# A hybrid decoder layer: where the halves of the projection's weights are stored

## The chip, the core and the metric

The program runs on one core of a Trainium2 chip. A core has a matrix engine (TensorE, PE in the rows, with its weight loads as PEld), a vector engine (VectorE, DVE), a scalar engine (ScalarE, ACT), GpSimd (POOL) and SyncE (SP), which in this kernel issues every DMA. Each engine runs its own list of instructions in order and waits for the others through semaphores. The metric is the device time of one execution in microseconds (us). Before the change it was 2645.74 us (median of 3 runs, 2643.93 to 2646.36).

## What is computed

One decoder layer over 2048 prompt rows and 8 sequences of 8 sample rows, all in float32, width 1024. Cut to its matrix products and what lies between them:

```
h   = rmsnorm(x, g_pre_mix)
z, q, k, v, glow, og = split(h @ w_in)              # 1024 x 2064
pool_out = pool_mixer(z, ...)                       # trailing windows 2, 4, 8, 16, minus z, per-group map
gla_out  = gla_mixer(q, k, v, log_sigmoid(glow @ w_gk2 + b) / 16, og, state)   # gated linear attention, chunks of 64
x   = x + rmsnorm(concat(pool_out, gla_out) @ w_o)
u, g = split(rmsnorm(x) @ w_up)                     # 1024 x 5632
x   = x + rmsnorm((gelu(causal_conv3(g)) * u) @ w_down)
x   = x + (p @ w_ple) * sigmoid(x @ w_ple_gate)
```

## The kernel before

The rows are cut into six tiles of 320, 384, 384, 384, 384 and 256 rows (tile 0 has 256 prompt rows and the 64 sample rows). The tiles go through the layer one after the other. A product of float32 accuracy is made from three matmuls (L1619, L1620, L1621): a matrix is split into a high half that TensorE takes exactly (`fp32r`) and a low half, the rest, and high*high, high*low and low*high are added up in PSUM.

The weights come as units of 128 partitions by 1024 words (512 KB), one for each block of 128 output columns. `UNITS` lists them all in the order in which TensorE takes them: for each tile 16 units `in` (in0 to in15), then, for the tile before, the first `ple` unit and three `gate` units, the eight `o` units, the second `ple` unit and five more `gate` units, 44 `up` units and 24 `down` units. Tile 0's `gate` units thus stand between tile 1's units. Four slots in SBUF hold the units; unit n goes to slot n % 4. A slot has two buffers: `stage`, over which `w_lo` lies in the same place, and `w_hi`.

For a plain unit SP loads the block into `stage`, ACT copies it to `w_hi` (L719, which rounds), DVE subtracts (L1133) and writes `w_lo` over `stage`, and TensorE waits for `lo_made`. For the 24 units `in` and `gate` of tile 0 both halves are then stored in DRAM (`kept_hi`, `kept_lo`), and all later tiles load the two halves in place of the block; for these units ACT and DVE have nothing to do, and TensorE waits for the landing of both (`halves_ready`).

SP's order is that of `load_unit(n)`. If the slot's former unit n-4 is to be kept, it first issues the two stores of that unit (`keep_unit`, L461 and L462); then it waits until TensorE has finished unit n-4 (`end_tick`, a count in `ticks`), then until the stores have landed (`keeping`), and only then issues the load of unit n. The stores of unit n-4 thus always go out right behind the load of unit n-1.

ACT and DVE go through the same list of units. At step n ACT first takes unit n-1's result out of PSUM (`finish`), then splits unit n+2 (`make_hi(n + 2)`), waiting for its landing, and only behind that does the step's own work: for tile units 3 to 9 `decay` (exponentials for one level of the attention's scores), at 9 and later `copy_v`, at 12 `copy_kd`, at the first `ple` unit `copy_out`, `square_out` and the evacuation of the `ple` results. DVE begins step n with `make_lo(n + 1)`. TensorE multiplies each level's operands (`scores`, L1678 and L1683) behind units in4 to in10, makes the chunks' states (`sum_state`, L1733) behind in12 and the chunks' outputs (L1748, L1754) behind in13 to in15.

Of the kernel before, what the change touches and what calls it, by code (L numbers as in the profile page):

```python
# [7 lines left out]
F32 = mybir.dt.float32  # L8
F32R = mybir.dt.float32r
U8 = mybir.dt.uint8  # L10
ALU = mybir.AluOpType
ACT = mybir.ActivationFunctionType

P = 128
D = 1024
KD = D // P
# [28 lines left out]
SLOTS = 4  # L45
# [15 lines left out]
def plan():  # L61

    units, outs, ticks = [], [], []

    def ple(t, s):
        units.append((t, "ple", s))
        for m in range(4 * s, 4 * s + 4):
            outs.append((t, "ple", m))
            ticks.append((t, "ple", m))

    def full(t, kind, m):
        for table in (units, outs, ticks):
            table.append((t, kind, m))

    for t in range(NT):
        for s in range(16):
            full(t, "in", s)
            if s >= 8 and s - 8 < chunks(t) + (TILES[t][2] > 0):
                outs.append((t, "v", s - 8))
        if t:  # L80
            ple(t - 1, 0)
            for m in range(EARLY_GATES):
                full(t - 1, "gate", m)
        for m in range(KD):
            full(t, "o", m)
        if t:
            ple(t - 1, 1)
            for m in range(EARLY_GATES, KD):
                full(t - 1, "gate", m)
        for m in range(2 * NF):  # L90
            full(t, "up", m)
        for m in range(3 * KD):
            units.append((t, "down", m))
            ticks.append((t, "down", m))
            if m % 3 == 0:
                outs.append((t, "down", m // 3))
    for s in range(2):
        ple(LAST, s)
    for m in range(KD):
        full(LAST, "gate", m)  # L100
    return units, outs, ticks


UNITS, OUTS, TICKS = plan()

KEPT = [unit for unit in UNITS if unit[0] == 0 and unit[1] in ("in", "gate")]
KEPT_NO = {unit[1:]: j for j, unit in enumerate(KEPT)}
HALVES = [unit[0] > 0 and unit[1:] in KEPT_NO for unit in UNITS]
SPLITS = list(itertools.accumulate(not halves for halves in HALVES))
UNIT_NO = {name: n for n, name in enumerate(UNITS)}  # L110
OUT_NO = {name: n for n, name in enumerate(OUTS)}
TICK_NO = {name: n for n, name in enumerate(TICKS)}
# [33 lines left out]
def hybrid_layer(nc, x_prompt, x_sample, state_pool, state_gla, state_conv, p_prompt, p_sample, packed,  # L146
# [4 lines left out]
    with ctx:  # L151
# [4 lines left out]
        def region(words):  # L156
            o = base[0]
            base[0] += (4 * words + 31) // 32 * 32
            assert base[0] <= top, (base[0], top)
            return o  # L160

        def at(name, shape, offset, dtype=F32):
            return nc.alloc_sbuf_tensor_at(name, shape, dtype, offset=offset)

        def own(name, shape, dtype=F32):
            n = mybir.dt.size(dtype)
            for s in shape[1:]:
                n *= s
            return at(name, shape, region((n + 3) // 4), dtype)
# [41 lines left out]
        slot_at = [region(KD * P) for _ in range(SLOTS)]  # L211
        stage = [at(f"stage{s}", [P, KD, P], slot_at[s]) for s in range(SLOTS)]
        w_lo = [at(f"w_lo{s}", [P, KD, P], slot_at[s], F32R) for s in range(SLOTS)]
        w_hi = [own(f"w_hi{s}", [P, KD, P], F32R) for s in range(SLOTS)]

        xr = [own(f"xr{n}", [P, KD, TM]) for n in range(2)]
        h_hi = own("h_hi", [P, KD, TM], F32R)
# [94 lines left out]
        def sem(name):  # L312
            return ctx.enter_context(nc.semaphore(name))
# [7 lines left out]
        landed = [sem(f"landed{s}") for s in range(SLOTS)]  # L321
        kept = [sem(f"kept{s}") for s in range(SLOTS)]
        hi_made, lo_made, ticks = sem("hi_made"), sem("lo_made"), sem("ticks")
# [71 lines left out]
        def exact(ap):  # L395
            return ap.bitcast(F32)
# [30 lines left out]

        def landing(n):

            return landed[n % SLOTS], 16 * sum(1 + HALVES[k] for k in range(n % SLOTS, n + 1, SLOTS))  # L430

        def keeping(n):
            return kept[n % SLOTS], 32 * sum(UNITS[k] in KEPT for k in range(n % SLOTS, n + 1, SLOTS))

        def tick(name):
            return ticks, TICK_NO[name] + 1
# [1 line left out]
        def end_tick(unit):  # L438
            t, kind, m = unit
            return tick((t, "ple", 4 * m + 3)) if kind == "ple" else tick(unit)  # L440

        def parts_of(unit):
            return DOWN_PARTS[unit[2] % 3][1] if unit[1] == "down" else KD
# [5 lines left out]
        def _(sp):  # L449
            def source(unit):  # L450
                t, kind, m = unit
                if kind == "down":
                    first_k, parts = DOWN_PARTS[m % 3]
                    return w_down_units[m // 3, :, first_k:first_k + parts, :]
                return {"in": w_in_units, "o": w_o_units, "up": w_up_units, "ple": w_ple_units,
                        "gate": w_gate_units}[kind][m]

            def keep_unit(n):
                s, j = n % SLOTS, KEPT_NO[UNITS[n][1:]]
                sp.wait_ge(lo_made, SPLITS[n])  # L460
                sp.dma_start(kept_hi[j], exact(w_hi[s][:, :, :])).then_inc(kept[s], 16)  # L461
                sp.dma_start(kept_lo[j], exact(w_lo[s][:, :, :])).then_inc(kept[s], 16)  # L462

            def load_unit(n):
                unit = UNITS[n]
                if n >= SLOTS:
                    if UNITS[n - SLOTS] in KEPT:
                        keep_unit(n - SLOTS)
                    sp.wait_ge(*end_tick(UNITS[n - SLOTS]))
                    if UNITS[n - SLOTS] in KEPT:  # L470
                        sp.wait_ge(*keeping(n - SLOTS))
                if HALVES[n]:
                    s, j = n % SLOTS, KEPT_NO[unit[1:]]
                    sp.dma_start(exact(w_hi[s][:, :, :]), kept_hi[j]).then_inc(landed[s], 16)
                    sp.dma_start(exact(w_lo[s][:, :, :]), kept_lo[j]).then_inc(landed[s], 16)
                    return
                dst = stage[n % SLOTS][:, 0:parts_of(unit), :]
                if unit[1] == "ple":
                    dst = dst.rearrange("p (k c) d -> p k (c d)", k=2)
                sp.dma_start(dst, source(unit)).then_inc(landed[n % SLOTS], 16)  # L480
# [36 lines left out]

            load_first_x()
            load_unit(0)
            sp.dma_start(const[:, 0:C_GK], packed[:, 0:C_GK]).then_inc(const_loaded, 16)  # L520
            load_unit(1)
            sp.dma_start(const[:, C_GK:C_ALL], packed[:, C_GK:C_ALL]).then_inc(tables_loaded, 16)
            load_unit(2)
            zs = state_pool[0].rearrange("b t (g c) -> (b t g) c", g=POOLG).rearrange("(q p) c -> p q c", p=120)
            sp.dma_start(z_state_tok[:, :, :], zs).then_inc(states_loaded, 16)
# [8 lines left out]
            for n in range(SLOTS, len(UNITS)):  # L534
                t, kind, m = UNITS[n]
# [169 lines left out]
        def _(act):  # L705
# [4 lines left out]
            def make_hi(n):  # L710
                for k in range(hi_next[0], min(n + 1, len(UNITS))):
                    one_hi(k)
                hi_next[0] = max(hi_next[0], n + 1)

            def one_hi(n):
                if n < len(UNITS) and not HALVES[n]:
                    s, parts = n % SLOTS, parts_of(UNITS[n])
                    act.wait_ge(*landing(n))
                    act.activation(w_hi[s][:, 0:parts, :], stage[s][:, 0:parts, :], ACT.Copy).then_inc(hi_made, 1)  # L719

            def root(out, ps, t, of=D):
                w = width(t)
# [247 lines left out]
            for n, (t, kind, m) in enumerate(UNITS):  # L970
# [78 lines left out]
                if kind == "up":  # L1049
                    f = m // 2  # L1050
# [64 lines left out]
        def _(dve):  # L1115
# [8 lines left out]
            def make_lo(n):  # L1124
                for k in range(lo_next[0], min(n + 1, len(UNITS))):
                    one_lo(k)
                lo_next[0] = max(lo_next[0], n + 1)

            def one_lo(n):
                if n < len(UNITS) and not HALVES[n]:  # L1130
                    s, parts = n % SLOTS, parts_of(UNITS[n])
                    dve.wait_ge(hi_made, SPLITS[n])
                    dve.tensor_tensor(w_lo[s][:, 0:parts, :], stage[s][:, 0:parts, :], exact(w_hi[s][:, 0:parts, :]),  # L1133
                                      ALU.subtract).then_inc(lo_made, 1)

# [334 lines left out]
            for n, (t, kind, m) in enumerate(UNITS):  # L1470
# [69 lines left out]
                if kind == "up":  # L1540
                    f = m // 2
# [60 lines left out]
        def _(pe):  # L1602
# [244 lines left out]
                y_turned.did(last, t, m)  # L1847

            def halves_ready(n):
                if HALVES[n]:  # L1850
                    pe.wait_ge(*landing(n))
                else:
                    pe.wait_ge(lo_made, SPLITS[n])

            def whole_unit(n, hi, lo, ready=None, between=None):
                t, kind, m = UNITS[n]
# [245 lines left out]
```

## Time and profile before

| | |
|---|---|
| median of the timed runs | 2645.74 us |
| the profiled execution's own time | 2644.32 us |
| its span in the trace | 2642.6 us |
| TensorE matmuls (PE) | 2579.1 us busy, 98% |
| weight loads (PEld) | 2515.4 us, 95% |
| VectorE (DVE) | 1581.9 us, 60% |
| ScalarE (ACT) | 1238.8 us, 47% |
| GpSimd (POOL) | 163.1 us, 6% |
| DMA | 428.54 MB, mean 162 GB/s |
| of it stored halves | 24 `kept_hi` and 24 `kept_lo`, 512 KB each |

How to read it: the span is one execution from first to last instruction. Busy shares are averages over stages that differ; a PE that is busy all the time may still run at half its clock, so the granted clock (PEclk, 1.00 is full) is read beside it. SPq is the queue on which SP issues DMAs; its rows begin when an instruction could be issued, after its waits. "idle 2.47 <-DVE ..." on a row says how long the engine stood still before it and what came last. Rows of the chain of waits follow the work that ended last back to its start.

### The profile page before, as it was taken

What the parts mean: (1) busy time and instruction counts of PE and PEld (TensorE: products, weight loads), DVE (VectorE), ACT (ScalarE), POOL (GpSimd) and SP (SyncE); (2) the same over time, 40 slices, a digit from 0 to 9 for tenths busy, and PEclk for the clock granted to TensorE, in tenths of its full rate; (3) what the DMA queues carried; (4) which work ended last, traced back from release to release, by engine and by line L of the source; (5) the groups of instructions that cost most, each with busy time, mean ns of one, the idle gap of its engine ahead of it and who ended that gap; (6) DMA issues with size and microseconds to landing.
All of it is one profiled execution on the core that took longest, in us unless ns stands there. A gap on an engine that the chain in (4) does not pass through costs nothing.

```text
span 2642.6 us, 41219 instructions
## 1 busy us (share of the span) xinstructions
PE 2579.1 (98%) x16510; PEld 2515.4 (95%) x16510; DVE 1581.9 (60%) x2539; ACT 1238.8 (47%) x2036; POOL 163.1 (6%) x492
## 2 busy tenths in 40 slices
PE   7889999998999999999999999999999999999998
PEld 6779999998999999999999999999999999999998
DVE  5557764647664464766546476644557664557864
ACT  3345553365444335544533654452355444356553
POOL 3201100100000010000001000000100000010000
PEclk9889999999999999999999999999999999999999
DMA  7633546446434544443454444345444434756566
GB/s 213 220 116 128 175 140 195 160 160 206 150 127 118 182 169 145 167 152 126 119 190 163 151 153 151 127 117 193 168 152 151 142 122 119 246 181 216 186 181 210
DMA packets 126564, 428.54 MB, mean 162 GB/s; under 512 B 13246, under 2 KB 21606, under 8 KB 126374
## 3 DMA queue, kind: packets, MB, share of 16 engines
q1 hardware_dynamic: 126374, 425.91, 49.1%
q8 instruction: 132, 2.16, 0.3%
q14 instruction: 58, 0.48, 0.1%
HBM read 390.38 MB, written 35.48 MB: 161 GB/s over the span
## 4 chain that ended last, share of the span: by engine, by line
PE 92%; DMA 3%; DVE 2%; ACT 1%; issue 1%; POOL 1%; SPq 0%; DVEq 0%; POOLq 0%
PE G L1619 28%; PE G L1620 28%; PE G L1621 28%; DMA kept_lo<-w_lo 2%; PE X L1678 2%; PE X L1612 1%; PE X L1615 1%; DMA stage<-in_w_up_units_dram 1%; PE X L1748 1%; PE X L1733 1%; PE X L1800 1%; DVE w_lo L1133 0%; PE X L1779 0%; PE X L1754 0%; PE G L1612 0%
## 5 line engine op out<-in xcount | busy, mean ns | idle before, releaser
L1619 PE MATMUL G<-h_hi,w_hi 128*128 128x384 f32 (+2 forms) x3264 | 1070.7, 328 | 23.5 <-DVE w_lo L1133 11.4
L1620 PE MATMUL G<-h_hi,w_lo 128*128 128x384 f32 (+2 forms) x3264 | 1053.5, 323 | 0.0
L1621 PE MATMUL G<-h_lo,w_hi 128*128 128x384 f32 (+2 forms) x3264 | 1053.3, 323 | 0.0
L719 ACT ACTIVATE w_hi<-stage 128x1024 fp32r<-128x1024 f32 (+1 forms) x492 | 510.5, 1038 | 485.5 <-DMA stage<-in_w_up_units_dram 253.3
L1133 DVE TENSOR_TENSOR w_lo<-stage,w_hi 128x1024 fp32r<-128x1024 f32 (+1 forms) x492 | 588.0, 1195 | 210.0 <-ACT w_hi L719 209.6
L1619 PEld LDWEIGHTS G<-h_hi,w_hi 128*128 128x128 f32 x3264 | 619.2, 190 | 32.6 <-DVE w_lo L1133 13.6
L1620 PEld LDWEIGHTS G<-h_hi,w_lo 128*128 128x128 f32 x3264 | 619.3, 190 | 1.0
L1621 PEld LDWEIGHTS G<-h_lo,w_hi 128*128 128x128 f32 x3264 | 618.7, 190 | 0.0
L1619 PE MATMUL G<-y_hi,w_hi 128*128 128x384 f32 (+2 forms) x1056 | 346.3, 328 | 0.0
L1621 PE MATMUL G<-y_lo,w_hi 128*128 128x384 f32 (+2 forms) x1056 | 339.6, 322 | 0.0
L1620 PE MATMUL G<-y_hi,w_lo 128*128 128x384 f32 (+2 forms) x1056 | 339.5, 321 | 0.0
L1395 DVE SCALAR_TENSOR_TENSOR cg<-gx,const,cg 128x384 f32<-128x384 f32 (+1 forms) x264 | 151.5, 574 | 88.3 <-ACT cg L878 63.8
L1619 PEld LDWEIGHTS G<-y_hi,w_hi 128*128 128x128 f32 x1056 | 199.1, 188 | 4.0 <-issue 2.9
L1620 PEld LDWEIGHTS G<-y_hi,w_lo 128*128 128x128 f32 x1056 | 199.2, 189 | 1.1
L1621 PEld LDWEIGHTS G<-y_lo,w_hi 128*128 128x128 f32 x1056 | 199.0, 188 | 0.0
L1383 DVE TENSOR_TENSOR gx<-G,rms_up 128x384 f32<-128x384 f32 (+1 forms) x132 | 67.6, 512 | 198.4 <-PE G L1621 183.4
L1141 DVE TENSOR_TENSOR total<-total,sq 128x384 f32<-128x384 f32 (+2 forms) x126 | 65.9, 523 | 155.3 <-ACT sq L732 154.3
L885 ACT ACTIVATE cg<-cg 128x384 f32<-128x384 f32 (+2 forms) x132 | 66.0, 500 | 173.7 <-DVE cg L1395 141.5
L732 ACT ACTIVATE sq<-G 128x384 f32<-128x384 f32 (+2 forms) x84 | 39.0, 465 | 216.3 <-PE G L1621 216.3
L1619 PE MATMUL G<-xg_hi,w_hi 128*128 128x384 f32 (+2 forms) x384 | 128.9, 336 | 3.7 <-DVE xg_lo L1434 2.3
L1620 PE MATMUL G<-xg_hi,w_lo 128*128 128x384 f32 (+2 forms) x384 | 124.1, 323 | 0.0
L1621 PE MATMUL G<-xg_lo,w_hi 128*128 128x384 f32 (+2 forms) x384 | 124.1, 323 | 0.0
(225 smaller groups left out, 2553.8 us busy)
## 6 DMA issues: line engine op xcount, KB each, us to landing
stage<-in_w_up_units_dram SPq DMA_DIRECT2D x264, 512.0 KB, 3.5
w_hi<-kept_hi SPq DMA_DIRECT2D x120, 512.0 KB, 3.7
w_lo<-kept_lo SPq DMA_DIRECT2D x120, 512.0 KB, 4.7
stage<-in_w_down_units_dram SPq DMA_DIRECT2D x96, 448.0 KB, 3.3
stage<-in_w_o_units_dram SPq DMA_DIRECT2D x48, 512.0 KB, 3.5
stage<-in_w_down_units_dram SPq DMA_DIRECT2D x48, 512.0 KB, 3.5
kept_hi<-w_hi SPq DMA_DIRECT2D x24, 512.0 KB, 5.3
kept_lo<-w_lo SPq DMA_DIRECT2D x24, 512.0 KB, 6.1
```

The source lines that it names most:

```text
L719: act.activation(w_hi[s][:, 0:parts, :], stage[s][:, 0:parts, :], ACT.Copy).then_inc(hi_made, 1)
L732: squared.did(act.activation(out[:, 0:width(t)], src[:, 0:width(t)], ACT.Square), t, m)
L885: gelu_made.did(act.activation(c[:, 0:w], c[:, 0:w], ACT.Gelu_apprx_tanh), t, f)
L1133: dve.tensor_tensor(w_lo[s][:, 0:parts, :], stage[s][:, 0:parts, :], exact(w_hi[s][:, 0:parts, :]), ALU.subtract).then_inc(lo_made, 1)
L1141: added.did(dve.tensor_tensor(start[:, 0:w], start[:, 0:w], ring[:, m % 2, 0:w], ALU.add), t, m - 1)
L1383: last = dve.tensor_tensor(x[:, 2:2 + np_], G[b][:, 0:np_], rms_up[:, 0:np_], ALU.mult)
L1395: last = dve.scalar_tensor_tensor(c[:, 0:np_], x[:, k:k + np_], tap, c[:, 0:np_], ALU.mult, ALU.add)
L1612: return pe.transpose(out, in_, ident[0:n, 0:n])
L1619: pe.matmul(ps[:, 0:w], l_hi, r_hi[:, 0:w], start=start, stop=False)
L1620: pe.matmul(ps[:, 0:w], l_lo, r_hi[:, 0:w], start=False, stop=False)
L1621: return pe.matmul(ps[:, 0:w], l_hi, r_lo[:, 0:w], start=False, stop=stop)
L1678: last = pe.matmul(X[first + b][:, col:col + 64], opnd[n % 2][r, d, cols(c)], queries[n % 2][r, d, 64 * c:64 * c + 64], start=True, stop=True)
```

## The change

In tile 0 the `in` units store only `w_lo`. In tile 1 the `in` units load the whole block (from `w_in`) and the stored low half; the block goes into a new name `w_whole` for the place of `w_hi`, ACT rounds it in place, and SP stores `w_hi` from there. Tiles 2 to 5 load two halves as before. The `gate` units keep both halves in tile 0 as before. TensorE waits in tile 1's `in` units for `hi_made` rather than for the landing.

```diff
-KEPT = [unit for unit in UNITS if unit[0] == 0 and unit[1] in ("in", "gate")]
-KEPT_NO = {unit[1:]: j for j, unit in enumerate(KEPT)}
-HALVES = [unit[0] > 0 and unit[1:] in KEPT_NO for unit in UNITS]
-SPLITS = list(itertools.accumulate(not halves for halves in HALVES))
+KEPT_NO = {unit[1:]: j for j, unit in enumerate(unit for unit in UNITS if unit[0] == 0 and unit[1] in ("in", "gate"))}
+KEEP_LO = [unit[0] == 0 and unit[1:] in KEPT_NO for unit in UNITS]
+KEEP_HI = [unit[1:] in KEPT_NO and unit[0] == (1 if unit[1] == "in" else 0) for unit in UNITS]
+
+LOADS_LO = [unit[0] > 0 and unit[1:] in KEPT_NO for unit in UNITS]
+LOADS_HI = [lo and not hi for lo, hi in zip(LOADS_LO, KEEP_HI)]
+HIS_MADE = list(itertools.accumulate(not loaded for loaded in LOADS_HI))
+LOS_MADE = list(itertools.accumulate(not loaded for loaded in LOADS_LO))
...
-        w_hi = [own(f"w_hi{s}", [P, KD, P], F32R) for s in range(SLOTS)]
+        hi_at = [region(KD * P) for _ in range(SLOTS)]
+        w_hi = [at(f"w_hi{s}", [P, KD, P], hi_at[s], F32R) for s in range(SLOTS)]
+        w_whole = [at(f"w_whole{s}", [P, KD, P], hi_at[s]) for s in range(SLOTS)]
...
-            def keep_unit(n):
-                s, j = n % SLOTS, KEPT_NO[UNITS[n][1:]]
-                sp.wait_ge(lo_made, SPLITS[n])
-                sp.dma_start(kept_hi[j], exact(w_hi[s][:, :, :])).then_inc(kept[s], 16)
-                sp.dma_start(kept_lo[j], exact(w_lo[s][:, :, :])).then_inc(kept[s], 16)
+            def keep_halves(n):
+                s, name = n % SLOTS, UNITS[n][1:]
+                if KEEP_HI[n]:
+                    sp.wait_ge(hi_made, HIS_MADE[n])
+                    sp.dma_start(kept_hi[KEPT_NO[name]], exact(w_hi[s][:, :, :])).then_inc(kept[s], 16)
+                if KEEP_LO[n]:
+                    sp.wait_ge(lo_made, LOS_MADE[n])
+                    sp.dma_start(kept_lo[KEPT_NO[name]], exact(w_lo[s][:, :, :])).then_inc(kept[s], 16)
...
-                if HALVES[n]:
+                if LOADS_LO[n]:
                     s, j = n % SLOTS, KEPT_NO[unit[1:]]
-                    sp.dma_start(exact(w_hi[s][:, :, :]), kept_hi[j]).then_inc(landed[s], 16)
+                    if LOADS_HI[n]:
+                        sp.dma_start(exact(w_hi[s][:, :, :]), kept_hi[j]).then_inc(landed[s], 16)
+                    else:
+                        sp.dma_start(w_whole[s][:, :, :], source(unit)).then_inc(landed[s], 16)
                     sp.dma_start(exact(w_lo[s][:, :, :]), kept_lo[j]).then_inc(landed[s], 16)
...
             def one_hi(n):
-                if n < len(UNITS) and not HALVES[n]:
+                if n < len(UNITS) and not LOADS_HI[n]:
                     s, parts = n % SLOTS, parts_of(UNITS[n])
+                    whole = w_whole[s] if LOADS_LO[n] else stage[s]
                     act.wait_ge(*landing(n))
-                    act.activation(w_hi[s][:, 0:parts, :], stage[s][:, 0:parts, :], ACT.Copy).then_inc(hi_made, 1)
+                    act.activation(w_hi[s][:, 0:parts, :], whole[:, 0:parts, :], ACT.Copy).then_inc(hi_made, 1)
...
             def halves_ready(n):
-                if HALVES[n]:
+                if LOADS_HI[n]:
                     pe.wait_ge(*landing(n))
+                elif LOADS_LO[n]:
+                    pe.wait_ge(hi_made, HIS_MADE[n])
                 else:
-                    pe.wait_ge(lo_made, SPLITS[n])
+                    pe.wait_ge(lo_made, LOS_MADE[n])
```

SP, tile 0, from the store of unit in0 to the load of in5, before (the number at the end of `w_hi`, `w_lo`, `stage` and `w_whole` tells the slot):

```order
L461 DMA kept_hi<-w_hi_72 128x1024
L462 DMA kept_lo<-w_lo_68 128x1024
L480 DMA stage_64<-in_w_in_units_dram 128x1024
L461 DMA kept_hi<-w_hi_73 128x1024
L462 DMA kept_lo<-w_lo_69 128x1024
L480 DMA stage_65<-in_w_in_units_dram 128x1024
```

SP at the same place in the changed kernel (its lines are numbered anew: L472 is the store of `w_lo`, L492 the load):

```order
L472 DMA kept_lo<-w_lo_68 128x1024
L492 DMA stage_64<-in_w_in_units_dram 128x1024
L472 DMA kept_lo<-w_lo_69 128x1024
L492 DMA stage_65<-in_w_in_units_dram 128x1024
L472 DMA kept_lo<-w_lo_70 128x1024
```

Between two loads one store stands where two stood; this holds 16 times. SP, tile 1, the loads of units in3 to in5, before:

```order
L474 DMA w_hi_75<-kept_hi 128x1024
L475 DMA w_lo_71<-kept_lo 128x1024
L474 DMA w_hi_72<-kept_hi 128x1024
L475 DMA w_lo_68<-kept_lo 128x1024
L474 DMA w_hi_73<-kept_hi 128x1024
```

The same place in the changed kernel:

```order
L486 DMA w_whole_79<-in_w_in_units_dram 128x1024
L487 DMA w_lo_71<-kept_lo 128x1024
L469 DMA kept_hi<-w_hi_72 128x1024
L486 DMA w_whole_76<-in_w_in_units_dram 128x1024
L487 DMA w_lo_68<-kept_lo 128x1024
L469 DMA kept_hi<-w_hi_73 128x1024
L486 DMA w_whole_77<-in_w_in_units_dram 128x1024
```

The two loads of in4, in5 and so on now stand behind a store of `kept_hi`, for whose landing they wait; the 16 stores stand before the loads of in4 to in15, of the first `ple` unit and of three `gate` units. ACT, tile 1, steps 11 to 13, before:

```order
L802 ACTIVATE v_tok<-G 128x512
L771 ACTIVATE Z<-G 128x384
L806 ACTIVATE kd_tok<-X 128x512
L809 ACTIVATE kd_tok<-X 128x256
L972 ACT_TABLE_LOAD
L776 ACTIVATE ogT<-G 128x384 x2
L719 ACTIVATE w_hi_72<-stage_64 128x1024
```

The same steps in the changed kernel:

```order
L732 ACTIVATE w_hi_73<-w_whole_77 128x1024
L815 ACTIVATE v_tok<-G 128x512
L784 ACTIVATE Z<-G 128x384
L732 ACTIVATE w_hi_74<-w_whole_78 128x1024
L819 ACTIVATE kd_tok<-X 128x512
L822 ACTIVATE kd_tok<-X 128x256
L985 ACT_TABLE_LOAD
L789 ACTIVATE ogT<-G 128x384
L732 ACTIVATE w_hi_75<-w_whole_79 128x1024
L789 ACTIVATE ogT<-G 128x384
L732 ACTIVATE w_hi_72<-stage_64 128x1024
```

ACT has a copy of 1024 words a partition in each of tile 1's steps (16 in all), and `kd_tok` of step 12 stands behind the copy of in14. TensorE, VectorE and GpSimd have the same instructions in the same order in both kernels.

## Rows read from the trace of the kernel before

**Rows 1.** The page: TensorE, and the shares of the chain that ended last.

```profile
PE 2579.1 (98%) x16510; PEld 2515.4 (95%) x16510; DVE 1581.9 (60%) x2539; ACT 1238.8 (47%) x2036; POOL 163.1 (6%) x492
PE 92%; DMA 3%; DVE 2%; ACT 1%; issue 1%; POOL 1%; SPq 0%; DVEq 0%; POOLq 0%
```

**Rows 2.** Waits of SP's queue: total us, times, longest.

```profile
SPq L471 <- DMA kept_lo<-w_lo: 138.6, 24, 7.0
```

**Rows 3.** The chain from 28 to 140 us: start, length, what.

```profile
61.04 0.33 SPq L480
...
61.89 6.15 DMA kept_lo<-w_lo
68.11 0.33 SPq L480
```

**Rows 4.** Timeline of SP in tile 0: the loads of in4 and in14.

```profile
32.09 0.33 SPq L480 DMA_DIRECT2D stage<-in_w_in_units_dram  x1
...
103.74 0.33 SPq L480 DMA_DIRECT2D stage<-in_w_in_units_dram  x1
```

**Rows 5.** Timeline of TensorE in tile 0: the waits behind 58 us.

```profile
68.72 1.11 PE L1678 MATMUL X<-queries,opnd 64*128 64x64 f32 x16 [1.06 <-DVE queries L1209]
...
76.01 1.08 PE L1678 MATMUL X<-queries,opnd 64*128 64x64 f32 x8 [2.47 <-DVE queries L1209]
...
89.54 0.44 PE L1619 MATMUL G<-h_hi,w_hi 128*128 128x320 f32 x1 [2.47 <-DVE w_lo L1133]
...
109.98 2.25 PE L1733 MATMUL X<-v_tok,kd_tok 128*128 128x256 f32 x5 [4.95 <-issue]
```

**Rows 6.** Busy us by stretch, then PEclk (granted), DMA share, GB/s.

```profile
57.00:95.00 38.00, 31.31 (x231) 29.01 (x231) 20.16 (x42) 11.92 (x24) 0.00 (x0) 0.87 0.67 232
95.00:127.60 32.60, 27.59 (x195) 25.52 (x193) 18.07 (x43) 11.22 (x21) 15.06 (x19) 0.95 0.63 203
127.60:149.30 21.70, 20.09 (x104) 17.88 (x103) 6.77 (x13) 12.44 (x25) 0.00 (x0) 0.69 0.48 167
...
443.00:514.00 71.00, 70.25 (x515) 67.26 (x515) 41.19 (x64) 22.83 (x48) 7.79 (x10) 1.00 0.58 199
```

**Rows 7.** Timeline of ACT in tile 0, step 12.

```profile
108.08 1.06 ACT L719 ACTIVATE w_hi<-stage 128x1024 fp32r<-128x1024 f32 x1 [4.96 <-DMA stage<-in_w_in_units_dram]
...
109.52 0.36 ACT L809 ACTIVATE kd_tok<-X 64x256 f32<-64x256 f32 x1
```

**Rows 8.** DMA issues in 33:80, 125:170, 465:515 and 443.1:447.3 us: KB, us to landing.

```profile
kept_lo<-w_lo SPq DMA_DIRECT2D x7, 512.0 KB, 6.1
...
stage<-in_w_o_units_dram SPq DMA_DIRECT2D x7, 512.0 KB, 3.5
...
w_lo<-kept_lo SPq DMA_DIRECT2D x8, 512.0 KB, 4.7
...
w_lo<-kept_lo SPq DMA_DIRECT2D x1, 512.0 KB, 6.4
```

**Rows 9.** Timeline of SP in tile 1: loads of in3, in4 and the second gate unit.

```profile
443.17 0.32 SPq L474 DMA_DIRECT2D w_hi<-kept_hi  x1
443.54 0.43 SPq L475 DMA_DIRECT2D w_lo<-kept_lo  x1
447.34 0.32 SPq L474 DMA_DIRECT2D w_hi<-kept_hi  x1
...
527.59 0.33 SPq L480 DMA_DIRECT2D stage<-in_w_gate_units_dram  x1
```

**Rows 10.** Timeline of TensorE in tile 1: the chunks' states, the last quarter of `ple`.

```profile
514.75 2.75 PE L1733 MATMUL X<-v_tok,kd_tok 128*128 128x256 f32 x12
...
538.79 0.42 PE L1619 MATMUL G<-p_hi,w_hi 128*128 128x320 f32 x1 [0.98 <-ACT ple L924]
```

**Rows 11.** Timeline of ACT in tile 1: end of step 12, and the second gate unit's split.

```profile
511.28 0.38 ACT L809 ACTIVATE kd_tok<-X 128x256 f32<-128x256 f32 x1
...
533.88 1.05 ACT L719 ACTIVATE w_hi<-stage 128x1024 fp32r<-128x1024 f32 x1
```

More of the change, by code:

```diff
@@ L428, in landing @@
         def landing(n):
-            return landed[n % SLOTS], 16 * sum(1 + HALVES[k] for k in range(n % SLOTS, n + 1, SLOTS))
+            return landed[n % SLOTS], 16 * sum(1 + LOADS_LO[k] for k in range(n % SLOTS, n + 1, SLOTS))
         def keeping(n):
-            return kept[n % SLOTS], 32 * sum(UNITS[k] in KEPT for k in range(n % SLOTS, n + 1, SLOTS))
+            return kept[n % SLOTS], 16 * sum(KEEP_LO[k] + KEEP_HI[k] for k in range(n % SLOTS, n + 1, SLOTS))
         def tick(name):
@@ L466, in load_unit @@
                 if n >= SLOTS:
-                    if UNITS[n - SLOTS] in KEPT:
-                        keep_unit(n - SLOTS)
+                    keep_halves(n - SLOTS)
                     sp.wait_ge(*end_tick(UNITS[n - SLOTS]))
-                    if UNITS[n - SLOTS] in KEPT:
+                    if KEEP_LO[n - SLOTS] or KEEP_HI[n - SLOTS]:
                         sp.wait_ge(*keeping(n - SLOTS))
-                if HALVES[n]:
+                if LOADS_LO[n]:
                     s, j = n % SLOTS, KEPT_NO[unit[1:]]
-                    sp.dma_start(exact(w_hi[s][:, :, :]), kept_hi[j]).then_inc(landed[s], 16)
+                    if LOADS_HI[n]:
+                        sp.dma_start(exact(w_hi[s][:, :, :]), kept_hi[j]).then_inc(landed[s], 16)
+                    else:
+                        sp.dma_start(w_whole[s][:, :, :], source(unit)).then_inc(landed[s], 16)
                     sp.dma_start(exact(w_lo[s][:, :, :]), kept_lo[j]).then_inc(landed[s], 16)
@@ L1129, in one_lo @@
             def one_lo(n):
-                if n < len(UNITS) and not HALVES[n]:
+                if n < len(UNITS) and not LOADS_LO[n]:
                     s, parts = n % SLOTS, parts_of(UNITS[n])
-                    dve.wait_ge(hi_made, SPLITS[n])
+                    dve.wait_ge(hi_made, HIS_MADE[n])
                     dve.tensor_tensor(w_lo[s][:, 0:parts, :], stage[s][:, 0:parts, :], exact(w_hi[s][:, 0:parts, :]),
@@ L2095 @@
     for name in ("kept_hi", "kept_lo"):
-        args.append(nc.dram_tensor(name, (len(KEPT), P, KD, P), F32, kind="Internal").ap())
+        args.append(nc.dram_tensor(name, (len(KEPT_NO), P, KD, P), F32, kind="Internal").ap())
     for n, shape in enumerate(_OUTS):
```

## The prediction, as it was put on record

> **What bounds the kernel now.** I read the page first, then SP's waits, then the chain of waits in the first 150 us, then the timelines of tile 0's and tile 1's `in` units, engine by engine.
>
> TensorE is busy 98% of the span and holds 92% of the chain; DMA holds 3% of it [rows 1]. A change that takes nothing from TensorE can therefore only move the stretches where it stands still or runs slowly. SP waits 24 times for the landing of a stored low half, 138.6 us in all, 5.8 us each [rows 2]; 16 of these are in tile 0. The chain shows one turn: the load at 61.04, both stores right behind it, the low half's issue at 61.89, 6.15 us to its landing, the next load at 68.11 [rows 3]. So a turn is one load, two stores and a landing, about 7.0 us, and each load waits for the one before to turn. From in4's load to in14's are ten turns, 71.65 us [rows 4].
>
> TensorE follows at that pace in the second part: it waits 1.06, 2.47, 2.47 and 4.95 us [rows 5]. The row that calls the last one "issue" can be resolved: ACT was held by the landing of in14 until 108.08, and `kd_tok`, which TensorE needs for the chunks' states, comes right behind that split and ends at 109.88 [rows 7]. So a late load costs more than its own unit: all that ACT has behind the split is late with it. Around these waits the granted clock is 0.87 and 0.95, that is, part of the time at the lower of the two levels (1.2 GHz for 2.4) [rows 6]. In tile 1 the same stage has a granted clock of 1.00 and 70.25 of 71 us busy [rows 6]: its loads are issued as soon as a slot is free.
>
> **The change in tile 0: what it gives.** 16 stores of 512 KB leave, so a turn is one load and one store. No row shows that pair. From below: one load alone lands in 3.5 us, two loads 0.37 us apart land in 0.37 + 4.7 = 5.1 us [rows 8, 9]. From above: the present turn of 7.0. The step from one transfer to two is 1.6 us, that from two to three 1.9. With the mean of these steps above 3.5, and 0.05 us for SP, the new turn is 5.3 us; that is the value I take, since the row of two transfers is the nearest. Ten turns and 0.6 us for a slower first one put in14's load at 32.09 + 0.6 + 53 = 85.7, and the states may begin 6.24 us behind it (109.98 - 103.74 [rows 4, 5]), at 91.9.
>
> What is late next is TensorE itself. Until the second level's scores (58 us) it waits for DVE's cumulative sums and the diagonal, which the change doesn't touch. Behind that, its waits are 1.06 + 2.47 + 2.47 + 4.95 = 10.95 us [rows 5]. The clock's share is 38 x 0.13 = 4.9 us and 32.6 x 0.05 = 1.6 us, since work at a granted clock of g takes 1 - g of the stretch too long [rows 6]. If both go wholly, TensorE comes to the end of in15 17.5 us sooner. The states would then begin near 93.8 (109.98 less 10.95, less 4.9, less the 0.4 or so of the second stretch that lies ahead of them), which is later than 91.9, so the loads allow it. I take 17 us, with 0.5 left for waits of ACT and DVE that the loads hide now. The bounds: 0 if the turn stays at 7.0, 17.5 at most. The stretch from 127.6 to 149.3, at 0.69, are the sample rows' small matmuls; it moves as a whole and stays slow. GpSimd's windows and SP's stores of states hang on the same ticks and move along.
>
> **The change in tile 1: what it costs.** ACT gets 16 copies of 1.05 us [rows 11], 16.8 us, in a stage where it is busy 22.8 of 71 us [rows 6]; that alone is hidden. What isn't hidden is SP's new order: behind the loads of in3 there is a store before each pair of loads, and the pair waits for its landing. A turn is two loads and one store. From below: two loads land in 5.1, and one more transfer costs 1.6 to 1.9 us, so 6.7; from above, the present 7.0 of one load and two stores. I take 6.85. Before, these loads were issued every 4.2 to 6.3 us, on TensorE's ticks.
>
> The start: in3's loads go out at 443.17, the store right behind. The pair's second load landed 6.4 us after 443.54 [rows 8, 9], behind the queue of its predecessors; the store, in the place of the next pair, lands about then, so in4's loads go out at 450.3 rather than 447.34. From there:
> - in14's loads: 450.3 + 10 x 6.85 = 518.8. They land in 5.1; the split takes 1.05, the two `kd_tok` copies 1.0 and the hand-over 0.15: the states begin at 526.1 rather than 514.75 [rows 10], 11.4 us late. ACT's `kd_tok` of 511.28 [rows 11] stands behind the split of in14 now; that is the costliest link.
> - the `ple` unit's load is 12 turns behind in4's, the second `gate` unit's two more, of one load and one store each: 450.3 + 82.2 + 10.6 = 543.1 rather than 527.59 [rows 9]. It lands in about 4.0 us (3.5 alone [rows 8]; 108.08 - 103.74 = 4.3 beside two stores [rows 4, 7]); from the start of its split to the last quarter of `ple` are 538.79 - 533.88 = 4.9 us of ACT's list [rows 10, 11]. So that quarter begins at 552.0 rather than 538.79: 13.2 us late.
>
> TensorE's own work between the two places took 538.79 - 0.98 - 514.75 = 23.1 us before [rows 10]. From 526.1 it comes to the same quarter at 549.2, or 550.7 with 1.5 us at the lower clock behind the wait, less than 552.0. Behind it, the rest of the layer is as before. The loss is 13.2 us. Its bounds: at turns of 6.65 and 5.1 it is 10.4, at 7.0 and 6.0 it is 16.4.
>
> At the stores a rule can be weighed. The rows show that a third transfer costs 1.9 us when it is a store and a second costs 1.6 when it is a load [rows 3, 8]. The Trainium skill, "DMA: Bandwidth & Descriptors", section "Anatomy of one DMA", says that a DMA has a fixed part of about 2 us, most of it the receipt of the write, and that this can be surprisingly long where HBM is written. By that rule one store keeps its long receipt and saves only bytes; the turns would be 5.45 and 7.0, the gain still 17 and the loss 15.3 us, which speaks against the change. The rows bear the rule out only weakly.
>
> **Sum.** 2644.32 - 17 + 13.2 = 2640.5 us for an execution like the profiled one. That one was 1.4 us under the median of the timed runs, so the forecast is 2645.74 - 3.8 = 2641.9, about 2642 us. What a measurement of this kernel can tell from no change is about 0.2%, 5.3 us; the forecast lies inside it. The change mostly moves a stall from tile 0 to tile 1.
>
> **Rivals.**
> - *Tile 1 hardly pays.* The price of a turn may be that of its two stores rather than of its three transfers; with one store it would be 6.2 us, and 4.7 with one load and one store. Then the second `gate` unit's load goes out at 450.3 + 74.4 + 9.4 = 534.1, the quarter begins at 543.0, the loss is 4.2 and the time 2645.7 - 17.5 + 4.2 = 2632.4. For it: stores land later than loads. Against it: two loads alone already take 5.1 us, and the steps of 1.6 and 1.9 are nearly even.
> - *Slower: the clock falls in tile 1.* TensorE would wait there for over 2 us several times, as it did in tile 0, and behind such waits the rows show the lower level. If it ran from 526.1 to the last quarter of `ple` at the 0.69 that the row of 127.6 to 149.3 shows, 23.1 us of work would take 33.5: the quarter begins at 559.6, the loss is 20.8, the time 2645.7 - 17 + 20.8 = 2649.5. It decides as soon as that work takes over 25.9 us, a mean under 0.89; with waits and a lower clock ahead of 526.1 as well it goes to 2652 or more. Against it: in tile 0 the stretches with waits kept 0.87 and 0.95, and what ran at 0.69 were matmuls with few columns.
> - *The single store's landing is mostly fixed.* If a load and a store turn in 6.2 us, in14's load in tile 0 goes out at 94.7, the states begin at 100.9 rather than 93.8, and the gain is 10.4; tile 1's turns of 7.0 and 6.2 make the loss 16.8. The time is 2645.7 - 10.4 + 16.8 = 2652.1. Against it: two loads in 5.1.
> - That the change isn't carried out can be left aside: the order of the instructions shows it.
>
> **How the numbers follow.** Forecast 0.52, its own range 2637 to 2647 (gain 15 to 17.5, loss 10 to 16); tile 1 hardly pays 0.20; clock 0.14; fixed landing 0.14. Faster by over 0.2% (under 2640.4) is all of the second case and a third of the first, 0.37; slower by over 0.2% (over 2651.0) is half of the clock's, over half of the fixed landing's and a little of the first, 0.17; within 0.2% is the rest, 0.46. The range of 8 in 10 reaches to both sides' cases: 2633 to 2652.
>
> **What would show it.** In tile 0 the loads stand 5.3 us apart (5.1 to 5.5) until TensorE's ticks set them, in15 ends 17 us sooner and the granted clock of that stage is over 0.97. In tile 1 the loads from in4 on stand 6.7 to 7.0 us apart; ACT waits for `w_whole`'s landing nearly every step; TensorE waits in front of in10 or in11 and for several us in front of the chunks' states. The last quarter of tile 0's first `ple` unit begins 4 us sooner than now, near 535, and from there the two traces keep that distance. A turn under 6.4 us in tile 1, or over 5.9 in tile 0, or a clock under 0.9 between 440 and 540 us would make the forecast wrong.

## The result, and the profile after

The changed kernel takes 2656.81 us (median of 5 runs, 2654.15 to 2658.99), the kernel before 2646.36 (median of 5). The ratio is 1.0036, with a 95% interval from 1.0026 to 1.0047: slower by about 10 us (7 to 12). The forecast was 2642, faster by some 4 us, with a range of 2633 to 2652, so both the sign and the range were missed. The profiled execution took 2654.15 us, its span is 2652.4 us, 9.8 more than before.

The page of the changed kernel, in the form of [rows 1]:

```profile
PE 2586.5 (98%) x16510; PEld 2522.3 (95%) x16510; DVE 1582.5 (60%) x2539; ACT 1255.1 (47%) x2052; POOL 162.5 (6%) x492
PE 90%; DMA 5%; DVE 2%; ACT 1%; issue 1%; SPq 1%; POOL 1%; DVEq 0%; POOLq 0%
```

DMA's share of the chain went from 3% to 5%. Waits of SP's queue in the changed kernel (total us, times, longest), against [rows 2]:

```profile
SPq L480 <- DMA kept_lo<-w_lo: 125.7, 24, 6.4
SPq L480 <- DMA kept_hi<-w_hi: 89.3, 16, 7.0
```

The 24 waits for low halves are 13 us shorter, and 16 waits of 5.6 us each have come in. Both stages can then be followed turn by turn. The first two rows are from SP's timeline, the loads of in4 and in14 in tile 0, against [rows 4]; the rest is the chain of waits in tile 1 (start, length, what):

```profile
31.57 0.33 SPq L492 DMA_DIRECT2D stage<-in_w_in_units_dram  x1
...
91.57 0.33 SPq L492 DMA_DIRECT2D stage<-in_w_in_units_dram  x1
```

```profile
431.85 7.40 DMA kept_hi<-w_hi
439.32 0.33 SPq L486
...
440.17 6.24 DMA kept_hi<-w_hi
446.47 0.33 SPq L486
...
505.79 6.37 DMA kept_hi<-w_hi
512.22 0.33 SPq L486
```

In tile 0 ten turns take 60.0 us: the first 7.0, the seventh 6.8, the other eight 5.7 to 5.8. Before, ten turns took 71.65. In tile 1 in4's loads go out at 439.32 and in14's at 512.22: 7.29 us a turn. What SP waited for between 440 and 540 us (total us, times, longest) is the stores' landing in nearly every turn:

```profile
SPq L480 <- DMA kept_hi<-w_hi: 77.4, 14, 6.3
SPq L486 <- PE G L1634: 0.7, 2, 0.4
```

TensorE's waits in both stages (timeline; the bracket at the end of a row is the wait before it), against [rows 5, 10]:

```profile
81.10 0.39 PE L1632 MATMUL G<-h_hi,w_hi 128*128 128x320 f32 x1 [1.31 <-DVE w_lo L1146]
...
97.98 2.26 PE L1746 MATMUL X<-v_tok,kd_tok 128*128 128x256 f32 x7 [2.66 <-issue]
...
456.69 2.15 PE L1691 MATMUL X<-queries,opnd 64*128 64x64 f32 x24 [3.16 <-DVE queries L1222]
...
520.13 5.46 PE L1746 MATMUL X<-v_tok,kd_tok 128*128 128x256 f32 x12 [3.75 <-issue]
...
547.65 0.42 PE L1632 MATMUL G<-p_hi,w_hi 128*128 128x320 f32 x1 [1.61 <-ACT ple L937]
```

The chunks' states of tile 0 begin 12.0 us sooner (97.98 against 109.98). The last quarter of `ple` in tile 1 begins 8.9 us later (547.65 against 538.79): between the two, 20.9 us are lost. At tile 1's states the wait is again that for `kd_tok` behind the split of in14 (timeline of ACT), against [rows 7, 11]:

```profile
518.22 1.06 ACT L732 ACTIVATE w_hi<-w_whole 128x1024 fp32r<-128x1024 f32 x1 [5.40 <-DMA w_lo<-kept_lo]
...
519.66 0.38 ACT L822 ACTIVATE kd_tok<-X 128x256 f32<-128x256 f32 x1
```

The stretches of [rows 6] in the changed kernel (busy us by engine, then the granted clock, DMA share, GB/s):

```profile
57.00:83.00 26.00, 24.22 (x213) 22.61 (x214) 18.40 (x38) 10.15 (x22) 0.00 (x0) 1.00 0.58 177
...
452.00:476.00 24.00, 20.84 (x109) 19.88 (x108) 13.25 (x23) 9.93 (x19) 0.00 (x0) 0.64 0.66 201
...
500.00:525.00 25.00, 19.93 (x116) 18.09 (x115) 12.82 (x18) 9.26 (x14) 10.37 (x11) 0.88 0.73 230
...
440.00:540.00 100.00, 90.10 (x575) 84.95 (x575) 50.56 (x85) 36.42 (x65) 10.37 (x11) 0.88 0.68 212
```

After the wait of 3.16 us at 456.69 TensorE ran for some 18 us mostly at 1.2 GHz (0.64 over the stretch). Before, tile 1's stage had 1.00 throughout.

### The profile page after: what moved, and what is told of

It reads as the page before. It is cut to its first block, busy times and chain, and to the rows that moved or that the text cites. A ratio compares the mean times of both kernels' runs of the same rounds, so it can differ in the third digit from the quotient of the medians.

```text
span 2652.4 us, 41251 instructions
## 1 busy us (share of the span) xinstructions
PE 2586.5 (98%) x16510; PEld 2522.3 (95%) x16510; DVE 1582.5 (60%) x2539; ACT 1255.1 (47%) x2052; POOL 162.5 (6%) x492
## 4 chain that ended last, share of the span: by engine, by line
PE 90%; DMA 5%; DVE 2%; ACT 1%; issue 1%; SPq 1%; POOL 1%; DVEq 0%; POOLq 0%
PE G L1632 28%; PE G L1634 27%; PE G L1633 27%; DMA kept_hi<-w_hi 2%; PE X L1691 2%; PE X L1625 1%; DMA kept_lo<-w_lo 1%; PE X L1628 1%; DMA stage<-in_w_up_units_dram 1%; PE X L1813 1%; PE X L1761 1%; PE X L1746 0%; DVE w_lo L1146 0%; PE X L1792 0%; PE X L1767 0%
```

## The experiments

**Do the two halves add?** Tile 0 alone (diffs are against the changed kernel unless said; "..." stands for lines left out, and in some only the new lines are printed). No tile stores the high halves of the `in` units, and the later tiles load the low half in their place, so that the number of transfers in each unit stays:

```diff
-KEEP_HI = [unit[1:] in KEPT_NO and unit[0] == (1 if unit[1] == "in" else 0) for unit in UNITS]
+KEEP_HI = [unit[1:] in KEPT_NO and unit[0] == 0 and unit[1] == "gate" for unit in UNITS]
...
-                        sp.dma_start(exact(w_hi[s][:, :, :]), kept_hi[j]).then_inc(landed[s], 16)
+                        sp.dma_start(exact(w_hi[s][:, :, :]), (kept_lo if unit[1] == "in" else kept_hi)[j]).then_inc(landed[s], 16)
```

> Tile 0's half of the change alone: the in units store only the low halves, and no tile stores or rebuilds the high ones (tiles 1 to 5 load the low half twice, so the high halves are left out of the product's values; transfers per unit are as before). If the two halves of the change simply add, this takes 12 us from before (the whole change's trace reached tile 0's first o unit 12.6 us sooner and its later units 12.2): 2634 us, with tile 1's loads on TensorE's ticks again. A rival, that the gain in tile 0 is given back by later waits in any case, expects 2640 or more. Turns of SP in tile 0: 5.75 us as in the whole change.

Measured: 2633.72 us against 2647.07, ratio 0.9952 (0.9937 to 0.9967), 13.4 us faster. The turns in tile 0 are 5.65 to 6.1 us behind a first one of 7.5.

Tile 1 alone:

```diff
-KEEP_HI = [unit[1:] in KEPT_NO and unit[0] == (1 if unit[1] == "in" else 0) for unit in UNITS]
+KEEP_HI = [unit[1:] in KEPT_NO and (unit[0] == 0 or unit[:2] == (1, "in")) for unit in UNITS]
```

> Tile 1's half alone: tile 0 stores both halves as before, tile 1 loads whole blocks and low halves, rounds, and stores the high halves again. If the halves add, 21 to 22 us over before: 2668 us, SP's turns in tile 1 7.3 us, tile 0 as before (turns of 7.0). If part of the loss came from tile 0 being sooner (transfers of tile 0 or the samples' outputs running into tile 1's), under 15.

Measured: 2670.03 us, ratio 1.0090 (1.0075 to 1.0105), 23.0 us slower; in4's loads to the first `ple` unit's are 12 turns of 7.5 us. The halves add: -13.4 + 23.0 = +9.6, and the whole change is +10.4; each of the two is known to some 4 us. So each term can be judged by itself.

**Which part of tile 1's half costs: ACT's copies or SP's wait?** The copies without the stores:

```diff
+KEEP_HI = [unit[1:] in KEPT_NO and unit[0] == 0 for unit in UNITS]
...
+LOADS_HI = [lo and unit[:2] != (1, "in") for lo, unit in zip(LOADS_LO, UNITS)]
```

> Tile 0 stores both halves as before; tile 1 loads whole blocks and low halves and ACT rounds them, but nothing is stored in tile 1. Theory: what costs is SP's turn (a load waits for the store that was issued behind the load before it); without it the loads go out on ticks again and ACT's 16 copies of 1.05 us are hidden: 2646 to 2649. Rival: ACT, which waits in its list for each landing and holds back the scores' exponentials, the values and kd_tok, costs by itself: 2655 or more.

Measured: 2647.39 us against 2647.07, ratio 1.0001 (0.9992 to 1.0011). Within some 2.5 us the 16 copies are free, and so is their place in ACT's list, as long as the loads come on time. The stores without the copies:

```diff
+KEEP_HI = [unit[1:] in KEPT_NO and (unit[0] == 0 or unit[:2] == (1, "in")) for unit in UNITS]
...
+LOADS_HI = LOADS_LO
...
-                    sp.wait_ge(hi_made, HIS_MADE[n])
+                    sp.wait_ge(*(landing(n) if LOADS_HI[n] else (hi_made, HIS_MADE[n])))
```

> Tile 0 as before; tile 1 loads both halves as before, ACT rounds nothing, but each unit's high half is stored again with the same wait for its landing. Theory of the turn: the loads in tile 1 are 7.2 to 7.3 us apart, the second gate unit's load is as late as in the whole change, and since its split stands in ACT's list ahead of the ple results, nearly the whole loss is there: 18 to 21 us over before, 2664 to 2668. Rival of ACT's held list in the in units: TensorE needs only the landing here, so under 10 us, 2656 or less.

Measured: 2671.61 us, ratio 1.0098 (1.0081 to 1.0114), 24.5 us slower, a little over the expected 18 to 21 as tile 1 alone was over it too (these compare with its 23.0). The whole loss is in the waits for the stores. This run also separates them from the clock. Its stretch of 440 to 540 us:

```profile
440.00:540.00 100.00, 92.56 (x637) 87.38 (x636) 47.13 (x80) 23.81 (x50) 12.02 (x15) 0.98 0.68 219
```

The granted clock is 0.98 here and 0.88 in the changed kernel, and the loss in tile 1 is no smaller.

**Why is a turn 7.3 us and not 6.85?** A load in the store's place (tiles 2 to 5 load the low half for the high half that isn't stored):

```diff
+        spare = own("spare", [P, KD, P])
...
+                    if name[0] == "in":
+                        sp.dma_start(spare[:, :, :], w_in_units[name[1]]).then_inc(kept[s], 16)
+                    else:
+                        sp.dma_start(kept_hi[KEPT_NO[name]], exact(w_hi[s][:, :, :])).then_inc(kept[s], 16)
...
-                        sp.dma_start(exact(w_hi[s][:, :, :]), kept_hi[j]).then_inc(landed[s], 16)
+                        sp.dma_start(exact(w_hi[s][:, :, :]), (kept_lo if unit[1] == "in" else kept_hi)[j]).then_inc(landed[s], 16)
```

> The whole change, but in tile 1 each store of a high half is replaced by a load of the same 512 KB into a spare buffer, issued at the same place and waited for in the same way (the stored high halves are thus left out, and tiles 2 to 5 load the low half in their place). Theory of the landing: a store ends 0.6 to 0.7 us later than a load whatever its bytes and holds up the loads beside it, so three loads turn in 5.1 + 1.55 = 6.6 to 6.7 us instead of 7.3, and the time is about 2648. Rival, the bytes or the three issues set the turn: 7.2 to 7.3 us and 2656 to 2657 as in the whole change.

Measured: 2645.73 us against 2646.69, ratio 0.9995 (0.9986 to 1.0005). Nine of the twelve turns from in4's loads on are 6.2 to 6.7 us, the other three 6.9 to 8.4, and their median is 6.6, against 7.3 with the store. So a store is dearer than a load. The DMA issues between 445 and 521 us (count, KB, median us to landing) show how. First the changed kernel, then this one:

```profile
w_whole<-in_w_in_units_dram SPq DMA_DIRECT2D x11, 512.0 KB, 4.1
w_lo<-kept_lo SPq DMA_DIRECT2D x11, 512.0 KB, 5.6
kept_hi<-w_hi SPq DMA_DIRECT2D x11, 512.0 KB, 6.3
```

```profile
spare<-in_w_in_units_dram SPq DMA_DIRECT2D x11, 512.0 KB, 5.5
w_whole<-in_w_in_units_dram SPq DMA_DIRECT2D x10, 512.0 KB, 3.6
w_lo<-kept_lo SPq DMA_DIRECT2D x10, 512.0 KB, 4.5
```

A third load leaves the two ahead of it as they were (3.6 and 4.5); a store behind them makes them later as well (4.1 and 5.6). The next two runs ask whether the store's price is a fixed part of its landing or in its bytes. An eighth of the store (here and in the next run tiles 2 to 5 again load the low half for the high one, as in the last hunk above):

```diff
+                    parts = 1 if name[0] == "in" else KD
+                    sp.dma_start(kept_hi[KEPT_NO[name]][:, 0:parts, :], exact(w_hi[s][:, 0:parts, :])).then_inc(kept[s], 16)
```

> The whole change, but tile 1 stores only the first eighth of each high half (64 KB; the rest is left out, and tiles 2 to 5 load the low half in its place). Theory of the landing: two loads and a store of almost nothing still turn in 5.1 + 0.65 + 0.2 = about 5.9 to 6.0 us where no tick is later (the loads of in5 to in8); the stage is then mostly on ticks and the time near that of tile 0's half alone, 2634 to 2639. Rival, a store's price is in its bytes: 5.3 to 5.4 us for the turn, 2634.

Measured: 2633.62 us, ratio 0.9950 (0.9935 to 0.9964). The same window:

```profile
w_whole<-in_w_in_units_dram SPq DMA_DIRECT2D x10, 512.0 KB, 3.7
w_lo<-kept_lo SPq DMA_DIRECT2D x10, 512.0 KB, 4.6
...
kept_hi<-w_hi SPq DMA_DIRECT2D x13, 64.0 KB, 4.3
```

Nine of the twelve turns are 5.1 to 5.5 us, the others 5.8 to 6.7; the median of 5.3 is little over the 5.1 that two loads alone take, so the theory of a long fixed landing, which wanted 5.9 to 6.0, fell. Half of the store (`parts = KD // 2`):

> The whole change, but tile 1 stores only the first half of each high half (256 KB; the rest is left out, and tiles 2 to 5 load the low half in its place). With an eighth stored the turns were 5.15 to 5.5 us, with all of it 7.3. If a store's price beside two loads is in its bytes (about 2.1 us for 448 KB more): turns of 6.1 to 6.2 us. If a store of some size brings the loads beside it to a slower pace at once (a switch rather than a slope): 6.7 or more.

Measured: 2638.15 us against 2646.99, ratio 0.9967 (0.9951 to 0.9983), turns of 5.9 to 6.2 us, but for the start (6.6) and one of 7.1. The same window as above:

```profile
w_lo<-kept_lo SPq DMA_DIRECT2D x10, 512.0 KB, 5.0
kept_hi<-w_hi SPq DMA_DIRECT2D x12, 256.0 KB, 5.2
```

The price grows with the bytes: the median turn is 5.3, 6.1 and 7.3 us at 64, 256 and 512 KB, and the second load beside the store lands in 4.6, 5.0 and 5.6 us. And the store with nothing beside it:

```diff
+                    if name[0] == "in":
+                        sp.wait_ge(*landing(n + SLOTS - 1))
```

> The whole change, but in tile 1 SP waits for the landing of the two loads before it issues the store, so that loads and store never run together. Theory of mixed traffic (a store and loads slow each other): the loads land as early as without stores (3.6 and 4.6 us), the store by itself in 3.5 to 3.9 us like a load, a turn is 5.1 + 3.9 + 0.5 for SP = 9.0 to 9.5. Theory of the direction (a store is slower whatever runs beside it): the store by itself takes 4.3 us or more, and a turn 9.7 or more. The time is long either way, 2680 to 2700.

Measured: 2663.89 us against 2646.99, ratio 1.0057 (1.0032 to 1.0083), well under the 2680 to 2700 expected. SP's timeline shows one turn, and the DMA issues between 435 and 521 us the landings:

```profile
437.81 0.33 SPq L488 DMA_DIRECT2D w_whole<-in_w_in_units_dram  x1
438.19 0.42 SPq L489 DMA_DIRECT2D w_lo<-kept_lo  x1
442.94 0.32 SPq L471 DMA_DIRECT2D kept_hi<-w_hi  x1
445.61 0.33 SPq L488 DMA_DIRECT2D w_whole<-in_w_in_units_dram  x1
```

```profile
kept_hi<-w_hi SPq DMA_DIRECT2D x11, 512.0 KB, 2.6
w_whole<-in_w_in_units_dram SPq DMA_DIRECT2D x11, 512.0 KB, 3.6
w_lo<-kept_lo SPq DMA_DIRECT2D x11, 512.0 KB, 4.5
```

By itself the store lands in 2.6 us (nine of twelve; the other three in up to 4.8), sooner than a load of the same size (3.5). Both theories had the store's lone landing too long, and eleven of the twelve turns came out at 7.45 to 8.8 us, not at 9.0 or more; one took 9.7. What the run does show is that 5.1 us of loads and 2.6 of store make a median turn of 7.8 one after the other and 7.3 together: beside loads a store hides only some 0.5 us of itself.

**The round trip taken away.** The stores of unit n-3 are issued ahead of the load of n rather than behind it. On the kernel before:

```diff
-                    if UNITS[n - SLOTS] in KEPT:
-                        keep_unit(n - SLOTS)
+                    for k in range(0 if n == SLOTS else n - SLOTS + 1, n - SLOTS + 2):
+                        if UNITS[k] in KEPT:
+                            keep_unit(k)
```

> The kernel before, with the two stores of a kept unit issued one load earlier (ahead of the load of n+3 instead of behind it), so that the load of n+4 waits for stores that went out a whole turn before. Theory: the turn is a round trip, not bandwidth (1.5 MB in 7.0 us are 224 GB/s, and tile 1's pairs ran at 3.1 us a MB): tile 0's loads go out on TensorE's ticks, 17 us less there, and a few more behind the stores of the gate units in tile 1: 2625 to 2631. Rival, the DMA engines are full: the turns stay near 7 us, 2644 or more.

Measured: 2618.71 us against 2646.69, 28 us less, ratio 0.9898 (0.9881 to 0.9914). TensorE begins tile 0's `o` units at 129.92 rather than 149.28, 19.4 us sooner, and the rest comes from behind the `gate` units' stores in tile 1. On the changed kernel (`keep_halves(k)` in the same loop):

> The changed kernel with the same earlier issue of its stores. Theory: with the round trip hidden both stages run on ticks; ACT's 16 copies cost nothing, as in the run without the stores in tile 1: 2625 to 2632, the same as the kernel before with the earlier issue within 3 us, and no store pattern is worth more than the other. Rival: 1.5 MB a turn is too much beside tile 1's units of 4.2 to 6.3 us, and the loss stays by half or more: 2640 or more.

Measured: 2617.79 us, ratio 0.9894 (0.9879 to 0.9909), the fastest version, though not told apart from the last one. Both gains are larger than I expected (2625 to 2631 and 2625 to 2632). Its two stages (busy us, granted clock, DMA share, GB/s) and SP's waits:

```profile
57.00:95.00 38.00, 38.00 (x315) 35.96 (x314) 29.21 (x51) 19.98 (x38) 9.02 (x6) 1.00 0.64 203
420.00:540.00 120.00, 118.27 (x812) 111.83 (x811) 68.30 (x113) 64.62 (x111) 12.04 (x15) 1.00 0.77 255
```

```profile
SPq L481 <- DMA kept_hi<-w_hi: 26.0, 12, 4.1
SPq L481 <- DMA kept_lo<-w_lo: 20.5, 9, 5.3
```

The same bytes pass at 255 GB/s in tile 1's stage while TensorE is busy 118 of 120 us at full clock; the waits for stores fell from 215 us in 40 waits to 46.5 in 21. Neither bandwidth nor ACT bounds the stage, only the order in which SP issued and waited.

## Why the prediction was wrong, step by step

*The place.* It named both round trips, tile 0's and the new one in tile 1, and the way in which they reach TensorE (`kd_tok` behind the split of in14, the second `gate` unit's split ahead of the `ple` results). The traces show both, and the two runs with half the change show that they add. That ACT's 16 copies are hidden was right: 2647.39 against 2647.07.

*The step that failed* is the price of a turn with one store in it, which sizes both terms of the sum. I took "the step from one transfer to two" as 1.6 us and "from two to three" as 1.9, whatever its direction, and put a turn at 5.3 us for a load and a store and 6.85 for two loads and a store. Measured: 5.75 and 7.3. The first store beside loads costs 2.2 us (3.5 to 5.75, and 5.1 to 7.3), a further load 1.5 to 1.6, and the second store of a pair only 1.25 (5.75 to 7.0). So the change takes away the cheap store of a pair in tile 0 and adds the dear one in tile 1. That asymmetry is what I didn't have. [Rows 3, 8] held a weak sign of it: a turn of 7.0 for a load and two stores lies 0.3 over the 6.7 that two steps of 1.6 from a load's 3.5 would give, and I spread the excess over the steps.

*The gain* was put at 17 us and is 13.4 by itself, 12.0 in the trace of the whole change. The prediction had in14's load at 85.7, so that TensorE, ready at 93.8, would be the later of the two. The load went out at 91.57, and 6.4 us on the states begin, at 97.98: the loads set their start, not TensorE. Of the 5.9 us by which that load is late, eight turns at 5.77 rather than 5.3 are 3.7 and the longer first and seventh turns 1.1 and 1.5; the stage began 0.5 sooner. Why those two turns are long isn't shown; the seventh was the longest but the first before the change too (7.6 us).

*The loss* was put at 13.2 and is 20.9 in the whole change, 23.0 alone. The second `gate` unit's load went out at 538.21. Counted from the shift of 12.2 us with which tile 1 now begins, the prediction had 543.1 - 12.2 = 530.9. Of the 7.3 us between them, 12 turns of 7.30 for 6.85 are 5.4, two of 5.65 for 5.3 are 0.7, and the start 1.2: in4's loads went out at 439.32, not 438.1, since the first store's landing took 7.4 us. The rest up to 20.9 is the unit's own landing (4.5 us for 4.0) and rounding.

*The rule* that I weighed is from the Trainium skill, "DMA: Bandwidth & Descriptors", section "Anatomy of one DMA": most of a DMA's fixed 2 us is the write's receipt, the longest where HBM is written. The section is written for DMAs that GpSimd issues, and here SP issues them, which the prediction didn't say. By the rule I had estimated turns of 5.45 and 7.0, nearer to the measured ones than mine, but not for its reason: an eighth of a store leaves the turn at 5.3 us, and a store alone lands in 2.6, sooner than a load's 3.5. The measurement decides here: the price is in the bytes of mixed traffic.

*The rivals.* "Tile 1 hardly pays" is refuted: its turn is the longest of all. "The landing is mostly fixed" forecast a loss of 16.8 and a time of 2652.1, near the outcome, by a cause that the small store refutes. The clock's rival was half right: TensorE did fall to 0.64 in one stretch and to 0.88 over 440 to 540 us, and a clock under 0.9 there was the one sign against itself, of the three that the prediction named, that turned up (its marks for the turns were over 5.9 us in tile 0 and under 6.4 in tile 1). But the clock isn't what the time was lost to. SP waited for TensorE only 0.7 us in that stretch and 77.4 for stores, and with the stores alone the loss was 24.5 us at a granted clock of 0.98.

*What stays open:* by what means a store makes the loads ahead of it land later, why the second store of a pair is cheap, and single long turns, such as those of 8.15 and 8.36 us in the run of tile 1 alone, whose stores took 7.2 and 7.4 us to land.

## What to carry to other kernels

A queue that issues "load, store, wait for the store, load" makes each load a round trip. Before moving bytes from one stage to another, see how long before its wait the store could have been issued: moving it ahead by one load gave 28 us here, where moving the bytes cost 10. When transfers of both directions share a turn, price them from a row with that mixture; where none exists, take as an upper bound one direction after the other (here 5.1 + 2.6 = 7.7 for a measured 7.3), not a mean of steps. No row from before the change had the 2.6; it takes a run with the store by itself.

## What the runs showed of the hardware

- A store of 512 KB with nothing beside it landed in 2.6 us, a load of the same size in 3.5.
- Beside two loads, the store cost about 2.2 us of the turn and made the loads themselves later, from 3.6 and 4.5 to 4.1 and 5.6 us; a third load in its place cost some 1.5 us and left them as they were.
- The price of the store followed its bytes: a median turn of 5.3, 6.1 and 7.3 us with 64, 256 and 512 KB stored behind two loads.
- TensorE stayed for some 18 us mostly at the lower clock (1.2 GHz; 0.64 granted over 452 to 476 us) after a wait of 3.16 us.
